# Loading x a second time in transposed form, and normalising the input projection at its two ends

## The reference

```
h = rmsnorm(x, ln_mix_g)          # x * 1/sqrt(mean(x*x) + eps) * gain, per token
z = h @ w_in                      # [c_q 384 | c_kv 256 | k_rope 32 | u 512]
y_mix = concat(mla(c_q, c_kv, k_rope), fourier_mix(u))
x = x + y_mix @ w_out
x = x + memory_xattn(rmsnorm(x, ln_x_g), mem, ...)
x = x + swiglu(rmsnorm(x, ln_ffn_g))
y = rmsnorm(x, final_norm_g)
```

## Time and profile before

| what | value |
|---|---|
| time, median of 3 runs | 1482.73 us (1482.49 to 1485.37) |
| time of the profiled execution | 1484.8 us |
| its span in the profile | 1483.0 us |
| mean granted clock | 0.987 |
| TensorE busy | 1399.0 us, 94% of the span |
| VectorE, ScalarE, GpSimd busy | 854.2, 670.1, 749.3 us |
| mean DMA rate | 108 GB/s |

### The profile page before, as it was taken

How to read it: one execution, slowest core, us unless ns; L and a number is a source line. 1 busy time by engine, 2 the same in 40 slices (tenths; PEclk the granted TensorE clock), 3 DMA queues, 4 the chain that set the end, 5 groups by cost and what they waited for, 6 DMA issues and landing times. The chain is left out here.

```text
span 1483.0 us, 19206 instructions
## 1 busy us (share of the span) xinstructions
PE 1399.0 (94%) x6928; PEld 1174.8 (79%) x6928; DVE 854.2 (58%) x1187; ACT 670.1 (45%) x1299; POOL 749.3 (51%) x595
## 2 busy tenths in 40 slices
PE   5998899999999988999999989999999999999986
PEld 4997678887889866888878768888888888888864
DVE  3567944316335599332243986666666664577985
ACT  4355855535324478445353633332323233444453
POOL 3433325951435422468415765555555553444895
PEclk9999999999999999999999999999999999999998
DMA  7211013631223200345125133333333225855323
GB/s 254 83 57 50 1 62 117 183 109 57 87 59 84 66 21 0 109 126 174 61 71 192 64 114 127 107 107 107 107 107 106 97 90 185 318 171 167 97 78 135
DMA packets 96697, 159.67 MB, mean 108 GB/s; under 512 B 8160, under 2 KB 41824, under 8 KB 96608
## 3 DMA queue, kind: packets, MB, share of 16 engines
q1 hardware_dynamic: 96032, 156.40, 32.5%
q10 hardware_dynamic: 576, 2.10, 0.4%
HBM read 129.89 MB, written 28.57 MB: 107 GB/s over the span
## 5 line engine op out<-in xcount | busy, mean ns | idle before, releaser
L669 POOL TENSOR_TENSOR w_lo<-w_raw,w_hi 128x512 fp32r<-128x512 f32 (+2 forms) x236 | 305.0, 1307 | 288.2 <-ACT w_hi L842 287.0
L842 ACT ACTIVATE w_hi<-w_raw 128x512 fp32r<-128x512 f32 (+2 forms) x236 | 140.5, 605 | 268.6 <-PE ps L1827 259.4
L1825 PE MATMUL ps<-h_hi_P,w_hi 128*128 128x512 f32 x616 | 241.3, 392 | 5.8 <-DVE h_lo_P L1275 3.1
L1827 PE MATMUL ps<-h_hi_P,w_lo 128*128 128x512 f32 x616 | 240.2, 390 | 0.0
L1826 PE MATMUL ps<-h_lo_P,w_hi 128*128 128x512 f32 x616 | 240.2, 390 | 0.0
L669 POOL TENSOR_TENSOR w_lo<-w_sum,w_hi 128x512 fp32r<-128x512 f32 x88 | 118.9, 1356 | 115.6 <-ACT w_hi L842 115.6
L669 POOL TENSOR_TENSOR w_lo<-a_raw,w_hi 128x512 fp32r<-128x512 f32 x77 | 113.4, 1474 | 81.5 <-ACT w_hi L842 81.5
L1825 PE MATMUL ps<-w_hi,act_hi 128*128 128x512 f32 (+1 forms) x384 | 140.7, 367 | 1.6 <-issue 1.6
L1825 PEld LDWEIGHTS ps<-h_hi_P,w_hi 128*128 128x128 f32 x616 | 116.0, 188 | 32.3 <-issue 4.7
L1827 PE MATMUL ps<-w_hi,act_lo 128*128 128x512 f32 (+1 forms) x384 | 140.1, 365 | 0.0
L1826 PE MATMUL ps<-w_lo,act_hi 128*128 128x512 f32 (+1 forms) x384 | 140.1, 365 | 0.0
(11 more groups left out here) (233 smaller groups left out, 3086.7 us busy)
## 6 DMA issues: line engine op xcount, KB each, us to landing
gu_raw<-in_w_gate_up SPq DMA_DIRECT2D x22, 1024.0 KB, 5.4
a_raw<-a_mem SPq DMA_DIRECT2D x77, 256.0 KB, 2.7
w_raw<-in_w_xkv SPq DMA_DIRECT2D x64, 256.0 KB, 3.0
a_mem<-down_sum SPq DMA_DIRECT2D x44, 256.0 KB, 2.5
wd<-in_w_down SPq DMA_DIRECT2D x44, 256.0 KB, 5.8
a_mem<-act_t SPq DMA_DIRECT2D x33, 256.0 KB, 2.1
w_raw<-in_w_out SPq DMA_DIRECT2D x32, 256.0 KB, 2.6
w_raw<-in_w_xq SPq DMA_DIRECT2D x32, 256.0 KB, 2.9
```

Of the source, the lines that this page charges most:

```text
L669: return nc.gpsimd.tensor_tensor(out, whole, hi.bitcast(F32), ALU.subtract)
L842: return nc.scalar.activation(out, in_, ACT.Copy)
L1825: nc.tensor.matmul(out, s_hi, m_hi, start=start, stop=False, skip_group_check=more)
L1827: return nc.tensor.matmul(out, s_lo, m_hi, start=False, stop=stop, skip_group_check=more)
```

## The change

x is also brought in transposed. The host supplies `x_t` (features by tokens) beside `x`, and the gain as `ln_cols`, a column of eight values per partition (`mix_gain`). `act_hi` is now made from `xt_raw` by ScalarE with the gain as scale (`column_hi`), and `act_lo` by VectorE as `xt_raw * gain - act_hi` (`column_lo`). The factor 1/rms per token is left out of the operand; it is applied when the results leave PSUM. For `z0` and `z1` the token is the partition, and the copy becomes a multiplication by `rstd[:, t]`. For `u` the token is the column, so a row of the factors is needed on every partition: four small fp32 products of `rstd`, spread over 128 columns, with the identity (`row_of_rstd`, before step 7 of `u`), copied to `rstd_row` by ScalarE. Stage `norm1` and its 32 transposes go. The product for `cw` moves from the program's start to between steps 0 and 1 of `z0` in group 0; `dft_hi`, `cw_hi`, `cw_lo` and `dft_lo` move behind it. For group 1 the columns are loaded and made during `xo1` of group 0. In group 1 the last normalisation into `h_tok` and its transposes stay.

```diff
-    order = [("norm1", 2 * T, None), ("u", 4, (w_in, KD, ZW, BANK)),
+    order = [("u", 4, (w_in, KD, ZW, BANK)),
 # SP, start
+            sp.dma_start(stats[:, 96:96 + KD], ln_cols[:, :]).then_inc(cols_in, 16)
+            for k in range(KD):
+                if k >= 4:
+                    sp.wait_ge(xt_in[k % 4], 16)
+                load_xt(0, k)
+                if k < RING:
+                    load_first_tile(k)
+                else:
+                    load_tile(0, k)
+                if 1 <= k <= T:
+                    t = k - 1
+                    sp.dma_start(x_res[:, t, :], x[0, t * P:(t + 1) * P, :]).then_inc(x_in[t], 16)
+                if k == 5:
+                    sp.dma_start(ident[:], tables[:, 0:P]).then_inc(ident_in, 16)
 # SP, in xo0 of group 0
-                        sp.dma_start(gain_n[:], ln_pair[g].partition_broadcast(P)).then_inc(gain_n_in, 16)
+                        if g == 0:
+                            for k in range(KD):
+                                if k >= 4:
+                                    sp.wait_ge(xt_in[k % 4], 16 * 3)
+                                load_xt(1, k)
 # POOL
-            pool.wait_ge(const_mid, 1)
-            sub(dft_lo[:], dft_raw[:], dft_hi[:]).then_inc(dft_ready, 1)
...
                     weights_lo(g, f"z{i}", 0, 4)
+                    if g == 0 and i == 0:
+                        pool.wait_ge(const_mid, 1)
+                        sub(dft_lo[:], dft_raw[:], dft_hi[:]).then_inc(dft_ready, 1)
                     odd_lo(g, 2 * i)
 # ACT
+            def column_hi(g, k):
+                act.wait_ge(xt_in[k % 4], 16 * (2 * g + k // 4 + 1))
+                if g > 0:
+                    wait_tile_used(act, g - 1, W["xo1"] + k)
+                nc.scalar.activation(act_hi[:, k, :], xt_raw[:, k, :], ACT.Copy,
+                                     scale=mix_gain[:, k:k + 1]).then_inc(xt_hi.sem, 1)
...
-                for f in range(KD):
-                    hi_out(g, TEN["norm1"] + f, act_hi[:, f, :], bank(TEN["norm1"] + f))
-                weights_hi(g, "u")
+                weights_hi(g, "u", KD - RING if g == 0 else 0, KD - 1)
+                act.wait_ge(row_full, g + 1)
+                copy(rstd_row[:], ps[:, ROW_BANK, :]).then_inc(row_copied, 1)
+                weights_hi(g, "u", KD - 1, KD)
...
-                weights_hi(g, "xo1")
+                for k in range(KD):
+                    weights_hi(g, "xo1", k, k + 1)
+                    if g == 0:
+                        column_hi(1, k)
 # DVE
+            def column_lo(g, k):
+                dve.wait_ge(xt_hi.sem, xt_hi.at(g, k + 1))
+                nc.vector.scalar_tensor_tensor(out=act_lo[:, k, :], in0=xt_raw[:, k, :], scalar=mix_gain[:, k:k + 1],
+                                               in1=act_hi[:, k, :].bitcast(F32), op0=ALU.mult,
+                                               op1=ALU.subtract).then_inc(xt_lo.sem, 1)
...
-                    nc.vector.tensor_copy(u_t[:, c, :], bank(ten)).then_inc(psum_free.sem, 1)
+                    nc.vector.tensor_tensor(u_t[:, c, :], bank(ten), rstd_row[:], ALU.mult).then_inc(psum_free.sem, 1)
...
-                        nc.vector.tensor_copy(z[:, t, i * ZP:(i + 1) * ZP], bank(ten, ZP)).then_inc(psum_free.sem, 1)
+                        if g == 0 and i == 0 and t == 0:
+                            dve.wait_ge(dft_ready, 1)
+                        nc.vector.tensor_scalar(z[:, t, i * ZP:(i + 1) * ZP], bank(ten, ZP), rstd[:, t:t + 1], None,
+                                                ALU.mult).then_inc(psum_free.sem, 1)
 # PE
-                transpose_features(g, TEN["norm1"], 0, h_tok, before={CW_BANK: lambda: pe.wait_ge(const_ready, 2)})
-                by_features(g, "u", act_hi, act_lo, S, split=TEN["norm1"])
+                def row_of_rstd():
+                    pe.wait_ge(ident_in, 16)
+                    pe.wait_ge(rstds.sem, rstds.at(g, 0))
+                    claim(g, ROW_BANK)
+                    for t in range(T):
+                        last = nc.tensor.matmul(ps[:, ROW_BANK, t * P:(t + 1) * P],
+                                                rstd[:, t:t + 1].broadcast_to([P, P]), ident[:], start=True, stop=True)
+                    last.then_inc(row_full, 1)
+                by_features(g, "u", act_hi, act_lo, S, first=True, before={KD - 1: row_of_rstd})
```

More of the change, by code:

```diff
@@ L194, in build @@
         h_tok = at("h_tok", R + 40, [P, T, D])
+        xt_raw = at("xt_raw", R + 40, [P, KD, S])
+        rstd_row = at("rstd_row", R + 56, [P, S])
         c_junk = at("c_junk", R + 70, [P, QR])
@@ L1403, in norm_x @@
                     normed(dst, x_res[:, g * T + t, :], t, gain).then_inc(h_ready.sem, 1)
-                for f in range(KD):
-                    ten = TEN["norm1"] + f
-                    lo_out(g, HI["norm1"] + f, ten, act_lo[:, f, :], bank(ten), act_hi[:, f, :])
+                dve.wait_ge(row_copied, g + 1)
                 for c in range(FG):
@@ L1415, in _ @@
                     butterflies(g, c)
+                if g == 0:
+                    for a in range(2):
+                        dve.wait_ge(cw_hi_done, a + 1)
+                        sub(cw_lo[:, :, a, :], ps[:, CW_BANK + a, :].rearrange("p (g d) -> p g d", g=FG),
+                            cw_hi[:, :, a, :]).then_inc(const_ready, 1)
                 for c in range(FG):
@@ L1855, in by_tokens, with by_features @@
                         last.then_inc(w_used.sem, 1)
-            def by_features(g, name, m_hi, m_lo, n, split=None, before=None):
+            def by_features(g, name, m_hi, m_lo, n, first=False, before=None):
                 for k in range(KD):
@@ L1864, in by_features @@
                         before[k]()
-                    if split is not None:
-                        pe.wait_ge(psum_free.sem, psum_free.at(g, split + k + 1))
+                    if first:
+                        pe.wait_ge(xt_lo.sem, xt_lo.at(g, k + 1))
                     for f in range(4):
-                        if k == 0:
+                        if k == 0 and first and g > 0:
+                            pe.wait_ge(psum_free.sem, psum_free.at(g, f - 4))
+                        if k == 0 and not first:
                             claim(g, TEN[name] + f)
@@ L1972, in fourier_positions @@
                     last.then_inc(psum_full.sem, 1)
-                by_tokens(g, "z0", act_hi, act_lo, T, before={4: lambda: fourier_channels(0),
+                by_tokens(g, "z0", act_hi, act_lo, T, before={**({1: channel_weights} if g == 0 else {}),
+                                                              4: lambda: fourier_channels(0),
                                                               6: lambda: fourier_channels(1)})
```

137 lines of the change are left out of this document (82 added, 55 removed).

## The result

The changed kernel takes 1473.77 us (median of 4 runs, 1472.16 to 1475.99), the kernel before beside it 1483.18 us (4 runs, 1482.49 to 1485.37). The ratio is 0.9935, with a 95% interval from 0.9918 to 0.9952. So the change is a gain of 9.4 us, and the forecast of 1465.9 us lies 7.9 us under the result, outside its range of 1463.3 to 1470.5. The profiled execution took 1474.04 us, its span is 1472.2 us: 10.8 us under the span before, where the sum said 16.8.

A forecast was written before the change was run, and what follows sets the result against it. TensorE, busy 94% of the span, was taken to bound the kernel. Gains of 15.1 and 3.2 less 1.5 gave 16.8 us off the profiled 1484.8, 1468.0; less 2.1 to the median, 1465.9 us, range 1463.3 to 1470.5.

The forecast's parts named there:

- the sum: Whole kernel: 15.1 - 1.5 + 3.2 = 16.8 us off the profiled execution, 1484.8 to 1468.0 us.
- term A: Start of group 0: `u` ends at 31.5 us instead of 46.56, gain 15.1 us, bounds 12 to 15.7.
- Its copy to `rstd_row` (0.65) lies beside step 7.: End of `u`, group 0: ScalarE's 0.65 us copy of the factors' row runs beside TensorE's step 7.
- A rival had named the weight stream behind `u`: Start's gain lost if weights behind `u` arrive no sooner; only 3.2 us stay, 1479.5 us; chance 2%.
- the cover on each step: Steps of `u`, group 0: operands are ready 2.1 to 2.5 us before TensorE needs them.
- the price of the row products: Before step 7 of `u`: four fp32 products of 128 columns add 1.0 us on TensorE.
- the 32 bytes per partition of gain columns: Start: ScalarE's first column waits for this small transfer and is somewhat later; no number changed for it.
- the low clock: First step of `u`, group 0: 3.3 us at half rate lose 1.65 us.
- Term B: Fourier constants inside `z0` of group 0: a loss of 1.5 us, bounds 0.8 to 4.4.
- VectorE's 9.7 us: `z0`, group 0: VectorE needs 8.39 + 1.29 = 9.7 us up to `v_lo`, against TensorE's 9.1.
- Term C: Boundary of the groups, `xo1` to `u`: 4.5 - 1.0 - 0.3 = 3.2 us gain, bounds 1.5 to 3.7.
- Everything behind `z0` moves as a whole: After `z0`: all later work shifts together, since it hangs on semaphores only.

The follow-up runs named there:

- late x: The changed kernel with the loads of group 1's x moved behind ScalarE's split of group 0's v: 1468.32 us, ratio 0.9895.
- copy first: The changed kernel with the copy to `rstd_row` ahead of ScalarE's last two weight splits of `u`'s stretch: 1471.94 us, ratio 0.9923.
- the second trace of after: The changed kernel run again with nothing edited: 1473.26 us, ratio 0.9924.
- late x and copy first: The changed kernel with group 1's x loaded after group 0's v split and `rstd_row` copied before the last two weight splits: 1468.79 us, ratio 0.9888.
- late x and warm: The changed kernel with group 1's x loaded after group 0's v split and three fp32 products of zeros on TensorE from about 1.9 us: 1466.82 us.
- warm: The changed kernel with three fp32 products of zeros on TensorE from 1.9 us on, nothing else: 1474.44 us, ratio 0.9934.

## Why the prediction was wrong

I take the steps by TensorE's lead over the trace before at five places: `z0` of group 0 (46.56 before), z's transposes (96.30), the end of `xo1` (416.06 + 0.23), `z0` of group 1 (442.64), and the end.

| lead in us at | forecast | after | late x |
|---|---|---|---|
| z0, group 0 | 15.1 | 11.8 | 14.0 |
| z's transposes | 13.6 | 8.9 | 13.2 |
| end of xo1 | 13.6 | 9.4 | 13.4 |
| z0, group 1 | 16.8 | 13.0 | 16.8 |
| end of the span | 16.8 | 10.8 | 16.8 |

**The step that failed** is in term A: "Its copy to `rstd_row` (0.65) lies beside step 7." I priced the copy and did not follow ScalarE's queue to it. I had done this for the columns of steps 2 to 5 and stopped there, and I followed the transfers to tile 7 only: its split began at 20.44 us, where I had the landing at 20.3. What came next in both queues decided: 2 MB of x on one, `dft_raw` and `c_gain` on the other, tile 12 behind them. From the last product of `u` to the first of `z0` stand 34.77 - 32.05 - 0.23 = 2.5 us that I had not.

A rival had named the weight stream behind `u`. I gave it 2% with the argument that a tile "lands within a few us of its issue". Those rows reach from 3.8 to 8.6 us, and their 8.6 is a tile of the very 2 MB in question, group 1's x. They could not bound a small tile that is issued behind nearly 3 MB. The rival's price was wrong as well: I let it cost the whole start, when it costs what the one late tile holds up.

**Right in term A**: the first product (6.95 forecast, 6.75 seen), the cover on each step (no idle inside `u`), the price of the row products (1.0 forecast, 0.9 seen: the second product behind them comes at 29.75 us, and 29.75 - 0.23 - 28.63 = 0.9). That the first column waits for the 32 bytes per partition of gain columns changed nothing: `ln_cols` landed 1.6 us after its issue. **Too narrow in term A**: the low clock. Products were 0.43 us apart from 6.75 to 12.46 us, which costs 2.8 us (half of 5.7) and not 1.65. I had taken one restart for the length. The same stretch, from the first product to the last at half rate, in the other runs that start cold: 4.9 us with late x (7.28 to 12.14), 3.6 with copy first (7.19 to 10.77), 3.2 in the second trace of after, 3.2 with late x and copy first (6.78 to 9.93). So 3.3 us was the lower end of what comes up, the cost lies between 1.6 and 2.8 us, and a single trace can't say which. The run with late x and warm gave back 2.5 us up to `z0` and 1.5 us of the whole. The lower bound of term A does not follow from its own terms either: a start at 9 us gives 46.56 - (9 + 21.87 + 1.65 + 1.0) = 13.0 us of gain, where the prediction has 12.

**Term B** was forecast at a loss of 1.5 us and cost 14.04 - 13.19 = 0.85 where the clock was full (late x), less than I took and just the lower bound of 0.8, TensorE's own addition less its idle: there was no wait for `v_lo` at all, `fourier_channels(0)` began 41.61 - 32.52 = 9.1 us after `z0`, exactly TensorE's own work. VectorE's 9.7 us was too slow by 0.6 us or more, because it took over the 8.39 us of the kernel before as they were. Two of the butterflies in them had met GpSimd, as VectorE's timeline of the kernel before shows:

```profile
50.83 1.15 DVE L1382 TENSOR_TENSOR u_t<-u_t 128x256 f32<-128x256 f32 x1
52.01 0.89 DVE L1384 TENSOR_TENSOR v_f<-u_t 128x128 f32<-128x128 f32 x1
```

Alone they take 0.42 and 0.29 us, as the others of their size do in the kernel after and with late x. With late x only one butterfly was stretched, to 1.03 us, and so was one more in the kernel before. These 1.3 us paid for `cw_lo`. In the changed kernel term B was 2.9 us. The difference is 2.0 us. Some 3.5 us at the clock of 0.50 behind the wait lose 1.7 of them. The other 0.3 lies in front of that: VectorE frees the four banks one by one, and the first ten products of `z0` take 36.47 - 34.77 = 1.7 us from the first to the tenth, where nine distances of 0.15 are 1.4. A wait of 2.5 us thus cost 4.5 in this trace. In the second trace it was less: there the constants' product, at 38.14 us, found the full clock again, and from `z0` to z's transposes it took 86.88 - 34.79 = 52.1 us against 50.6, 1.5 lost.

**Term C** was right: 3.2 us forecast, 12.96 - 9.43 = 3.5 seen, and again 442.64 - 430.86 less 8.25 = 3.5 in the second trace. VectorE's remainder did meet GpSimd's, as forecast. VectorE and GpSimd of the kernel after at this place, which answer to the earlier trace rows:

```profile
405.62 1.27 DVE L1363 SCALAR_TENSOR_TENSOR act_lo<-xt_raw,stats,act_hi 128x512 fp32r<-128x512 f32 x1 [1.45 <-ACT act_hi L989]
406.81 2.47 DVE L1455 TENSOR_TENSOR x_res<-ps,x_res 128x512 f32<-128x512 f32 x4
409.21 0.73 DVE L1363 SCALAR_TENSOR_TENSOR act_lo<-xt_raw,stats,act_hi 128x512 fp32r<-128x512 f32 x1
```

```profile
405.05 1.29 POOL L704 TENSOR_TENSOR w_lo<-w_raw,w_hi 128x512 fp32r<-128x512 f32 x1 [1.43 <-ACT w_hi L878]
```

1.27 us beside GpSimd, 0.73 alone. TensorE lost about 0.1 us by it at 407.55, since the first addition took 0.6 us.

**"Everything behind `z0` moves as a whole"** holds for the waits, not for the clock. The lead of the changed kernel fell from 13.0 to 10.8 us in the last part. These stretches are of TensorE's idle at 1407.55 and the work behind it, first of the kernel after:

```profile
1407.50:1413.00 5.50, 5.45 (x17) 4.39 (x18) 4.96 (x3) 2.59 (x6) 4.54 (x4) 0.69 0.37 95
```

then of the same kernel again, at its own time:

```profile
1408.30:1414.00 5.70, 5.22 (x22) 4.06 (x23) 5.70 (x4) 4.30 (x9) 5.70 (x4) 1.00 0.30 93
```

Both had idled 2.1 us just before. One went on at 0.69, the other at 1.00, from there to the next wait 19.2 against 18.2 us. The traces of warm and of late x with copy first show the long form, too; the other nine, of before among them, the short one. That is about half of the 2.2 us. The other 0.9 lie behind TensorE's idle of 5.84 us that ends at 1454.37: the clock of 0.50 lasts there until 1459.8 us, 5.4 us into the work, and only 3.6 us in the kernel before (1466.04 to 1469.6) and in the second trace (1454.27 to 1457.9). The same difference shows behind z's transposes: to the first scores it is 35.4 us in before, after and late x, and 36.5 in the second trace of after. What decides such a difference is not shown by these runs; it moves a single trace by 1 us at each such place and is not an effect of the change.

**The account** of the 6.0 us that the trace lacks against the sum: 3.3 at the start (2.5 wait, 1.1 more low clock, less 0.3 on the row products and the start), 1.4 in `z0` (2.0 behind the wait, less 0.65), 2.2 at the end, less 0.5 and 0.3 that came out better between and at the boundary. Of these 4.5 us are the wait and what follows from it; the low clock at the start and most of the loss at the end are what differs from trace to trace. Take the backlog away alone and the sum comes true to the tenth: late x has a span 16.8 us shorter, 1468.05 us profiled where I had 1468.0. To the tenth it is luck: in the table the start is 1.1 us short of the forecast, which the low clock of 4.9 us and the first product at 7.28 us explain, and term B, the stages behind it and term C make up for that with 0.7, 0.2 and 0.2. Between that and 1465.9 I had set the 2.1 us by which the profiled execution stood above the median of three runs. Over 15 runs before's median is 1483.7 to 1484.2, and the allowance should have been 0.6 to 1.1. That is 1 to 1.5 us of the miss which belongs to no engine.

## What to carry to other kernels

When an evacuation begins to need a new operand, follow the queue of the engine that makes it item by item, up to the last thing ahead of it, including splits whose data come by transfer; a price and a place "beside step 7" is not enough. When work is pulled forward, look at the transfers that were issued at leisure at the old time: here a prefetch that cost nothing before (1.0004) cost some 5 us after (1473.77 against 1468.32), and the cure was to issue it later. Behind a new wait of 2 to 3 us on TensorE another 1.5 to 2 us were lost here, most of it to the clock.

## What the runs showed of the hardware

- A 168 KB tile took 3.1 us from issue to landing, and 8.8 us with 2 MB more on another engine's queue. With these 2 MB on their way the small tile got no preference over the large ones that had been issued on the other queue up to 2 us earlier.
- GpSimd and VectorE slowed each other: a 128 x 256 butterfly from 0.42 to 1.12 us, a 128 x 512 `SCALAR_TENSOR_TENSOR` from 0.73 to 1.27, four of 128 x 1024 from 4.87 to 7.90 together, six remainders on GpSimd from 7.43 to 10.47. Letting GpSimd start as soon as its operands were there made a kernel some 3 us slower than holding it back.
- TensorE's first products ran at half rate for 3.2 to 5.7 us in five traces, busy without a break and with the same instructions; three products of zeros ahead of them, from 1.9 us on, took that away.
- After an idle of 2.1 us at the same instruction the granted clock fell to 1.2 GHz in 3 of 12 traces; of two traces of the changed kernel one shows it and one not.
- The plain fp32 product of two times 512 columns took 1.7 us at 2.4 GHz, and 2.9 us mostly at 1.2 GHz. The product behind it is recorded 0.4 us before it can run, so such a price is read from the second start behind it.
